# Seven block products for eight in three units of each down projection

## The reference

```python
def swiglu(x, w_gate, w_up, w_down):
    return (jax.nn.silu(x @ w_gate) * (x @ w_up)) @ w_down
...
    for layer in range(DEPTH):
        h = h + 0.5 * swiglu(rms_norm(h, ln_ffn1[layer]), ffn1_w_gate[layer],
                             ffn1_w_up[layer], ffn1_w_down[layer])
        ...                       # attention: differential in layer 0, sliding window in layer 1
        h = h + 0.5 * swiglu(rms_norm(h, ln_ffn2[layer]), ffn2_w_gate[layer],
                             ffn2_w_up[layer], ffn2_w_down[layer])
```

## Time and profile before

| what | value |
|---|---|
| median of 3 runs | 919.54 us |
| the profiled execution, its own time | 919.42 us |
| its span, first to last instruction | 917.6 us |
| TensorE, matmuls | 905.8 us busy, 99% |
| TensorE, weight loads (beside the matmuls) | 745.5 us, 81% |
| VectorE | 574.0 us, 63% |
| ScalarE | 471.6 us, 51% |
| granted clock of TensorE | 0.998 of full speed |
| HBM traffic | 220 GB/s over the span |

### The profile page before, as it was taken

The page is one execution under the profiler, slowest core; times in us unless marked ns, Lnnn a source line. Parts: engine busy times, 40 slices in busy tenths (PEclk is TensorE's granted clock), DMA queues, the critical chain, the costliest instruction groups (busy, mean ns, idle before and its releaser), DMA issues.

```text
span 917.6 us, 11621 instructions
## 1 busy us (share of the span) xinstructions
PE 905.8 (99%) x4195; PEld 745.5 (81%) x4195; DVE 574.0 (63%) x724; ACT 471.6 (51%) x635; POOL 90.7 (10%) x170
## 2 busy tenths in 40 slices
PE   8999999999999999999999999999999999999997
PEld 7888888888888888888888888888876788888885
DVE  5656663574787766665467566644588776656542
ACT  6554443565685654444346445433478664444431
POOL 1100005623311100000002000000030000000000
PEclk9999999999999999999999999999999999999999
DMA  9898778558733888876557888874563388887611
GB/s 306 258 296 240 240 243 243 209 180 289 234 98 93 263 266 261 246 261 230 178 162 231 251 249 249 301 243 171 196 230 110 121 279 272 263 252 285 228 71 46
DMA packets 169758, 202.86 MB, mean 221 GB/s; under 512 B 15160, under 2 KB 139136, under 8 KB 169712
## 3 DMA queue, kind: packets, MB, share of 16 engines
q1 hardware_dynamic: 168752, 201.37, 67.5%
q0 software_dynamic: 512, 0.36, 0.4%
q10 hardware_dynamic: 448, 0.53, 0.2%
HBM read 184.39 MB, written 17.83 MB: 220 GB/s over the span
## 4 chain that ended last, share of the span: by engine, by line
PE 91%; DVE 4%; DMA 2%; issue 1%; ACT 1%; SPq 1%; POOL 0%; POOLq 0%; DVEq 0%; ACTq 0%
PE bank L535 58%; PE bank L574 18%; PE bank L580 9%; PE bank L596 2%; PE bank L764 1%; PE bank L639 1%; DVE w_lo L1767 1%; PE bank L795 1%; DMA raw<-in_ffn_w_up 1%; DMA x_bounce<-silu 0%; PE bank L817 0%; PE bank L741 0%; SPq L1055 0%; ACT junk L1399 0%; DVE hT_lo L1767 0%
## 5 line engine op out<-in xcount | busy, mean ns | idle before, releaser
L1767 DVE TENSOR_TENSOR w_lo<-raw,w_hi 128x2048 fp32r<-128x2048 f32 x149 | 340.2, 2292 | 185.5 <-ACT w_hi L1380 185.1
L1380 ACT ACTIVATE w_hi<-raw 128x2048 fp32r<-128x2048 f32 x154 | 294.4, 1916 | 194.3 <-PE bank L580 97.6
L535 PE MATMUL bank<-w_hi,xT_hi 128*128 128x512 f32 x816 | 318.8, 391 | 0.2 <-DVE w_lo L1774 0.2
L535 PE MATMUL bank<-w_lo,xT_hi 128*128 128x512 f32 x816 | 317.6, 389 | 0.0
L535 PE MATMUL bank<-w_hi,xT_lo 128*128 128x512 f32 x816 | 307.9, 389 | 0.0
L535 PEld LDWEIGHTS bank<-w_hi,xT_hi 128*128 128x128 f32 x816 | 153.2, 188 | 33.1 <-DVE w_lo L1774 0.6
L535 PEld LDWEIGHTS bank<-w_hi,xT_lo 128*128 128x128 f32 x816 | 153.2, 188 | 31.9
L535 PEld LDWEIGHTS bank<-w_lo,xT_hi 128*128 128x128 f32 x816 | 153.2, 188 | 31.3
L574 PE MATMUL bank<-w_hi,hT_hi 128*128 128x512 f32 x348 | 135.6, 390 | 0.0
L574 PE MATMUL bank<-w_lo,hT_hi 128*128 128x512 f32 x348 | 135.4, 389 | 0.0
L580 PE MATMUL bank<-w_hi,hT_lo 128*128 128x512 f32 x348 | 107.1, 389 | 0.0
(11 more groups left out here) (182 smaller groups left out, 599.7 us busy)
## 6 DMA issues: line engine op xcount, KB each, us to landing
raw<-in_ffn_w_down SPq DMA_DIRECT2D x88, 512.0 KB, 5.1
raw<-in_ffn_w_gate SPq DMA_DIRECT2D x86, 512.0 KB, 5.9
raw<-in_ffn_w_up SPq DMA_DIRECT2D x86, 512.0 KB, 7.0
raw<-in_a_w_qkv SPq DMA_DIRECT2D x24, 512.0 KB, 5.6
h_bounce<-silu SPq DMA_DIRECT2D x40, 256.0 KB, 7.0
...
```

Of the source, the lines that this page charges most:

```text
L535: mm = nc.tensor.matmul(bank[b][:, :], xs[:, kt, own(pos)], ws[:, slot(u), cols], start=(kt == 0 and i == 0), stop=(kt == KT - 1 and i == 2))
L1380: nc.scalar.activation(w_parts(u)[0], raw[:, slot(u), :], ACT.Copy).then_inc(s_hi, 1)
L1767: nc.vector.tensor_tensor(lo, raw[:, slot(u), :], hi.bitcast(F32), ALU.subtract).then_inc(s_lo, 1)
```

## The change

In units i = 2, 4 and 6 of the down part the eight products become the seven of a Strassen scheme. Let A(pos, k) be the tiles of h. With S1 = A10 - A11, S2 = A00 - S1, S3 = A10 - A00, S4 = A01 - S2 and T1 = B00 + B01, T2 = T1 + B11, T4 = T2 + B10, T3 = T2 - B00 the seven products are A00 B00, S2 T2, S3 T3, S1 B01', A11 T4, A01 B10 and S4 B11, where B01' is T1: VectorE adds B00 onto B01 in `raw` (`t_first`), before the unit is split. Products shared by several outputs are summed over the three units in banks 4 to 7; three go to the usual banks. The pieces:
- The order of the down units is `DN_ORDER`; units go through TensorE one by one up to i = 6, each for both positions. The three units hold the first tiles of blocks 0, 1, 2.
- The four sums S come from `landed` in the loop turns g = 1 to 3 (`h_sum`, four instructions of 128x128, two of them followed by a wait for themselves), with a high part by ScalarE and a low part by VectorE, 128x512 each. In these turns and in turn 4 `h_hi` and `h_lo` of position 1 move ahead of split 4g+5, `h_sum` goes between them and the split.
- T2, T4, T3 (`t_sums`, 128x512 each) go where the low part of x was (`xT_lo`), so the first waits until the gate-up part is over; `t_high` (ScalarE) and `t_low` (VectorE) split them, 128x1536 in one instruction each. TensorE waits for `t_low` at the start of each seven.
- SyncE waits for `t_sums` before it loads over a unit that they read (units 28, 30, 32).
- `seven_added`: ScalarE copies bank 4, VectorE adds the four shared sums to x in eight instructions, behind split 32.
- The sums of h take the place of the three vectors (two biases, the final norm), which are now loaded at the end of the down part; two small tables move to `shared`.

```diff
+DN_ORDER = [1, 3, 0, 5, 2, 6, 4, 7, 8, 9, 10]
+SEVEN = [2, 4, 6]
...
+            def three(b, lhs, rhs, start=False, stop=False):
+                (l_hi, l_lo), (r_hi, r_lo) = lhs, rhs
+                nc.tensor.matmul(bank[b][:, :], l_hi, r_hi, start=start, stop=False)
+                nc.tensor.matmul(bank[b][:, :], l_hi, r_lo, start=False, stop=False)
+                return nc.tensor.matmul(bank[b][:, :], l_lo, r_hi, start=False, stop=stop)
+            def seven(f, u, n):
...
+                pe.wait_ge(s_h_sums_lo, seven_no(f, n))
+                pe.wait_ge(s_t_lo, seven_no(f, n))
+                for b in (4, 5, 6, 7) if begin else ():
+                    take(b)
+                three(6, s_tile(3), t_tile(T3), begin, end)
+                three(5, s_tile(2), t_tile(T2), begin, end)
+                three(acc(1, 0), a_tile(1, 1), t_tile(T4)).then_inc(s_t_used, 1)
+                unit_ready(u)
+                three(7, s_tile(1), b_tile(0, 1), begin, end)
+                three(4, a_tile(0, 0), b_tile(0, 0), begin, end)
+                three(acc(0, 0), a_tile(0, 1), b_tile(1, 0))
+                three(acc(0, 1), s_tile(4), b_tile(1, 1)).then_inc(s_used, 1)
...
-                down((0, 1, 2), 0)
+                down((0,), 0)
                 pe.wait_ge(s_hT_lo[1], block_no(f, H_BLOCKS - 2))
-                down((0, 1, 2), 1)
-                down((3, 4, 5, 6), 0)
-                down((3, 4, 5, 6), 1)
+                down((0,), 1)
+                for i in range(1, SEVEN_END):
+                    if i in SEVEN:
+                        seven(f, u0 + GU_UNITS + i, SEVEN.index(i))
+                    else:
+                        down((i,), 0)
+                        down((i,), 1)
...
# SyncE, loads of down units
+                        if i - UNITS_HELD in SEVEN:
+                            sp.wait_ge(s_t_sums, seven_no(f, SEVEN.index(i - UNITS_HELD)))
...
# ScalarE, a turn
                     split(u0 + 4 * g + 4, turn)
-                    split(u0 + 4 * g + 5, turn)
                     if g:
                         h_hi(1, g - 1, 0 if turn is None else turn)
-                    else:
+                    split(u0 + 4 * g + 5, turn)
+                    if not g:
                         act.wait_ge(s_rstd, rstd_count(name, 1))
                     silu_gate(1, 0, g, turn)
+                    if turn is not None:
+                        h_sums_high(f, turn)
...
# ScalarE, down part
-                split(u0 + 24)
+                split_with_t1(u0 + 24, f, 0)
                 split(u0 + 25)
                 silu_gate(1, 0, 5)
-                split(u0 + 26)
+                t_high(f, 0)
+                split_with_t1(u0 + 26, f, 1)
                 h_hi(1, 4)
-                for i in range(27, 30):
-                    split(u0 + i)
+                split(u0 + 27)
+                t_high(f, 1)
+                split_with_t1(u0 + 28, f, 2)
+                split(u0 + 29)
                 h_last_hi(0)
                 h_last_hi(1)
+                t_high(f, 2)
                 for i in range(30, 33):
                     split(u0 + i)
+                act.wait_ge(s_used, u0 + GU_UNITS + SEVEN_END)
+                nc.scalar.activation(p1_copy, bank[4][:, :], ACT.Copy).then_inc(s_read[4], 1)
...
# VectorE
+            def t_first(f, u, n):
+                dve.wait_ge(s_raw[slot(u)], 32 * (u // UNITS_HELD + 1))
+                nc.vector.tensor_tensor(raw_tile(u, 0, 1), raw_tile(u, 0, 1), raw_tile(u, 0, 0),
+                                        ALU.add).then_inc(s_t1, 1)
+            def t_sums(f, u, n):
+                if n == 0:
+                    dve.wait_ge(s_used, u - SEVEN[0])
+                else:
+                    dve.wait_ge(s_t_used, seven_no(f, n) - 1)
...
+                link(nc.vector.tensor_tensor(t2, raw_tile(u, 0, 1), raw_tile(u, 1, 1), ALU.add))
+                nc.vector.tensor_tensor(t4, t2, raw_tile(u, 1, 0), ALU.add)
+                nc.vector.tensor_tensor(t3, t2, raw_tile(u, 0, 0), ALU.subtract).then_inc(s_t_sums, 1)
...
# VectorE, a turn
                     split(u0 + 4 * g + 4, turn)
-                    split(u0 + 4 * g + 5, turn)
                     if g:
                         h_lo(1, g - 1, 0 if turn is None else turn)
+                    if turn is not None:
+                        h_sum(f, turn)
+                    split(u0 + 4 * g + 5, turn)
...
                     mul(1, 0)
+                    if turn is not None:
+                        h_sum_low(f, turn)
...
# VectorE, down part
                 turn_of(4)
+                t_first(f, u0 + 24, 0)
                 split(u0 + 24)
                 split(u0 + 25)
                 h_last_turned(0)
                 dve.wait_ge(s_turned[1], block_no(f, H_BLOCKS - 1))
                 mul(1, 0, 5)
                 h_last_turned(1)
+                t_sums(f, u0 + 24, 0)
+                t_first(f, u0 + 26, 1)
+                t_low(f, 0)
                 split(u0 + 26)
                 h_lo(1, 4)
-                for i in range(27, 30):
-                    split(u0 + i)
+                split(u0 + 27)
+                t_sums(f, u0 + 26, 1)
+                t_first(f, u0 + 28, 2)
+                t_low(f, 1)
+                split(u0 + 28)
+                split(u0 + 29)
                 h_last_lo(0)
                 h_last_lo(1)
+                t_sums(f, u0 + 28, 2)
+                t_low(f, 2)
                 for i in range(30, 33):
                     split(u0 + i)
+                seven_added(f)
```

More of the change, by code:

```diff
@@ L139, in trunk @@
         xT_hi = sb("xT_hi", [P, KT, SEQ], F32R)
+        with nc.sbuf_tensor("t_raw", [P, KT * SEQ], F32) as t_raw:
+            pass
         xT_lo = sb("xT_lo", [P, KT, SEQ], F32R)
@@ L206, in trunk @@
         gain_rows = shared[0:6 * KT, 1024:1024 + P]
+        p1_copy, p6_less = [silu[:, pos, :, :].rearrange("p j n -> p (j n)") for pos in range(NPOS)]
+        p5_more = h[:, 0, :]
         turned = [silu[:, pos, :, :].rearrange("p j n -> p (j n)") for pos in range(NPOS)]
@@ L558, in last_rows_pass, with rows_pass @@
                 mm.then_inc(s_used, 1)
-            def rows_pass(u, kt0, n_kt, pos, lhs_hi, lhs_lo, key, part=None, lo_ready=None):
+            def rows_pass(u, kt0, n_kt, pos, lhs_hi, lhs_lo, key, part=None, lo_ready=None, first=None):
+                if first is None:
+                    first = kt0 == 0 and part != 1
                 if pos == 0 and (u, part) == (U_WO_A + 3, 0):
@@ L565, in rows_pass @@
                     unit_ready(u)
-                if kt0 == 0 and part != 1:
+                if first:
                     take(acc(pos, 0))
@@ L574, in rows_pass @@
                             nc.tensor.matmul(bank[acc(pos, j)][:, :], lhs_hi[:, kt, own(pos)],
-                                             ws[:, slot(u), cols], start=(kt == 0 and i == 0), stop=False)
+                                             ws[:, slot(u), cols], start=(first and kt == kt0 and i == 0),
+                                             stop=False)
                     if k == 0 and lo_ready:
@@ L1113, in ffn @@
                 h_in(f, 0, 3)
-                for name in vectors:
-                    vector(name)
                 down(0, 1)
@@ L1129, in ffn @@
                     h_last_in(f, pos)
-                down(*range(8, DN_UNITS))
+                down(8, 9)
+                if "b_b_q" in vectors:
+                    vector("b_b_q", u0)
+                down(10)
+                for name in vectors:
+                    if name != "b_b_q":
+                        vector(name, u0)
             def rows(u0, n, w):
@@ new lines, in t_low, with h_sum, a_tile, s_raw_tile @@
+            def t_low(f, n):
+                dve.wait_ge(s_t_hi, seven_no(f, n))
+                cols = slice(0, 3 * BANK)
+                nc.vector.tensor_tensor(t_lo[:, cols], t_raw[:, cols], t_hi[:, cols].bitcast(F32),
+                                        ALU.subtract).then_inc(s_t_lo, 1)
+            def h_sum(f, turn):
+                def a_tile(pos, k):
+                    return landed[pos].rearrange("p (q t s) -> p t q s", q=4, t=4)[:, k, :, :]
+                def s_raw_tile(i):
+                    return vec[:, bass.ds(turn, 1), BANK + P * (i - 1):BANK + P * i].rearrange(
+                        "p o (q s) -> p (o q) s", q=4)
+                link(nc.vector.tensor_tensor(s_raw_tile(1), a_tile(1, 0), a_tile(1, 1), ALU.subtract))
+                link(nc.vector.tensor_tensor(s_raw_tile(2), a_tile(0, 0), s_raw_tile(1), ALU.subtract))
+                nc.vector.tensor_tensor(s_raw_tile(3), a_tile(1, 0), a_tile(0, 0), ALU.subtract)
+                nc.vector.tensor_tensor(s_raw_tile(4), a_tile(0, 1), s_raw_tile(2),
+                                        ALU.subtract).then_inc(s_h_sums, 1)
@@ new lines, in h_sum_low, with seven_added, counted, into_x @@
+            def h_sum_low(f, turn):
+                dve.wait_ge(s_h_sums_hi, turn + seven_no(f, 0))
```

(28 more changed lines are left out.)

61 lines of the change are left out of this document (53 added, 8 removed).

## The result

The changed kernel takes 940.95 us (median of 4 runs, 936.94 to 943.18) against 919.66 (918.83 to 919.99) for the kernel before beside it, a ratio of 1.0228 [1.0191, 1.0266]. It is slower, and far outside the predicted 912.5 to 927.0. The profiled execution took 942.12 us, span 940.3, mean granted clock 0.989. First the busy times and the chain, which answer to the earlier trace rows.

What follows compares the result with a forecast made beforehand. TensorE's matmuls were taken to bound the kernel (busy 99% of the span). 919.4 - 8.2 for matmuls saved + 1.7 loop turns + 6.3 first sevens + 2.8 later sevens = 922.0 us, range 912.5 to 927.0.

Steps and rivals of the forecast that it cites:

- What goes: Down projections: three units in four FFNs take 21 matmuls, not 24; 36 matmuls at 0.2267 us go, 8.16 us.
- What costs nothing: Down part: ScalarE's and SyncE's new waits, accumulators of banks 4 to 7 and `seven_added` hold up no matmul; no cost.
- first seven: Down part: serial chain behind the landing of position 0's block 4 makes `t_low` late, 6.3 us in all, 10 at most.
- rival 3: Clock falls at each first seven, 21 matmuls running at 1.2 GHz; adds 19 us, 941; chance 0.03.
- Loop turns: Gate-up part: low parts of 4g+5 and 4g+6 late behind the landing in FFN 1 and 3; 1.7 us, bounds 0 and 4.
- L: Gate-up turn: time from S to the landing of position 1's h bounce; 14.0 us in FFN 1, 14.8 in FFN 3.
- S: Start of a gate-up loop turn on TensorE, from which times are counted; a turn has 96 matmuls, 21.76 us.
- The drift: Gate-up loop: L of the next turn is L + 0.1, less the stall, so a delay is not worked off.
- D: End of the gate-up part, S + 27.2 in turn 4, 417.35 in FFN 1.
- second sevens: Down part: VectorE's rounds make second and third sevens late by 0.3 and 0.4 us, 2.8 us in four FFNs.
- The sum: Whole kernel: 919.4 - 8.2 + 1.7 + 6.3 + 2.8 = 922.0 us.
- rival 1: The h pipeline keeps up, L returns to 12 to 12.4; 914.0 us, up to 917.5; chance 0.34.

Runs made afterwards that it cites:

- e10: On e1: gate-up split 4g+5 back ahead of h_hi and h_lo, SyncE waiting for h_sum, high and low parts of the h sums moved later; 914.23 us.
- e1: Changed kernel, with the first two units of a down projection, not one, multiplied for position 0 before position 1 is begun on TensorE; 923.86 us.
- e4: Changed kernel with 12 more matmuls, which nothing waits for, ahead of TensorE's wait 12 matmuls into each down part; 931.51 us.
- e3: Kernel before, eight products in all units, with the first down unit multiplied for both positions before the next two are begun; 934.0 us.

## Why the prediction was wrong

**What goes: right.** The sevens run at 0.227 us, and with e10 the saving is there: 919.4 - 8.2 + 3.1 for the price left in the down parts - 1.3 in the stretches between the FFNs = 913.0; profiled 912.94.

**The step that failed** stands under "What costs nothing": it looked at the accumulators of banks 4 to 7 and not at those of position 1, whose take-over the new order on TensorE moves from the 37th to the 13th matmul. The chain it needed had been worked out for the first seven: splits 24 and 25, the turn of h, then the product. In the kernel before, that product comes behind the turn of h in the earlier trace rows:

```profile
421.57 0.44 DVE L1888 STREAM_TRANSPOSE h<-h 128x256 f32<-128x256 f32 x1
421.93 0.44 DVE L1863 SCALAR_TENSOR_TENSOR h<-bank,rstd,silu 128x256 f32<-128x256 f32 x1
```

It ends at 422.37, 5.2 us after the part's first matmul: well ahead of 36 matmuls (8.16) and well behind 12 (2.72). So 2.5 us four times could be read from the trace before, and 0.4 to 1.7 more with the later split 24. The prediction put this wait at nothing; it measured 14.2 us, and 7.4 more by the lower clock behind it, 21.6 us in all. The profiled executions of the changed kernel and of e1 are 19.3 us apart, as e1 keeps some 3 us of waits.

**The clock** was rival 3, with a chance of 0.03 and in another place. Its argument, that no wait of the trace before was followed by a fall, held only for waits as short as those of that trace. The wait had to be found first; with four waits of 3 to 4 us in the sum it would have been a term to price; in the changed kernel it came behind each of them. The Trainium skill (TensorE: Matmul & The Clock Gate, "HAM oscillation") says that idle gaps between matmuls bring the lower clock; the traces agree (granted clock 0.50 from 875 to 880 us, behind a wait of 4.12), and e4 puts some 7.6 us on it.

**Loop turns.** The mechanism was right: TensorE idle in the first loop turns behind the low parts of 4g+5 and 4g+6, with L + 5.0 for the L + 4.75 worked out. The size was not, 6.4 for 1.7. L was 15.7 in FFN 1, not 14.0, and 15.6 in FFN 3, not 14.8: in FFN 1 the write-out was issued 4.0 us after S, before 2.1, and the reads 12.2 after, before 10.6. In FFN 1 the delay begins ahead of the loop, where SyncE writes x to the scratch and reads it back for the norm of position 1. Before, then after:

```profile
299.14 0.34 SPq L1043 DMA_DIRECT2D x_bounce<-silu  x1
...
301.18 4.01 SPq L1055 DMA_DIRECT2D xn<-x_bounce  x8
...
303.60 0.34 SPq L1133 DMA_DIRECT2D x_bounce<-silu  x1
...
307.67 3.65 SPq L1145 DMA_DIRECT2D xn<-x_bounce  x8
```

This write landed after 4.1 us, before 2.0, so the reads came 2.0 us later in the part, and the requests behind them stayed some 1.7 us late. Where the reads came 3.71 us after the part's first matmul (before, e3, e4), L is 13.8 to 14.0; where they came at 4.9 to 5.7 (all others), 14.7 to 15.9. Why that write lands later is open; e4 shows that the changed kernel can have either. The drift did not come: L of the next turns is 13.25, 13.2 and 12.3, so a delay is worked off.

**The first seven.** It was predicted 6.3 us late in four; in the changed kernel it was in time, but only because TensorE had lost 5 us ahead of it. `t_low` ended 11.35 us after D in FFN 1 (D + 12.75 worked out). The chain was sized rightly, 15.2 us from the landing for the 15.1 worked out; but the landing came at D - 3.9, not D - 2.4, since L in turn 4 was 12.3 and not 13.85. In e1, without that loss, the waits before position 1 and the starts of the first sevens come to about 3 us. In the changed kernel the second sevens were in time and the third 0.37 us late, 1.5 us in four where 2.8 stood for both.

**The sum.** With e1's order the forecast of 922.0 meets 923.86, but by two errors of opposite sign: the loop 4.7 us too cheap (6.4 for 1.7), the down parts 3.4 too dear (5.7 for 9.1). The forecast was right about a kernel that had one more unit in front of position 1. That rival 1's 914.0 is so near e10's 914.23 is luck too: in e10 the first landings are as late as ever (L 15.7 in FFN 1, 15.3 in FFN 3), and its time needed three moves.
